# A two-block network on one core: the expert layers' token state made in the weights' feature order, its three bf16 parts written without a step

## The reference, cut to what matters

```python
# block 1
hx = _modulate(_rms_norm(x, g_pre_ffn[l]), mx[3], mx[4])
x = x + mx[5] * _rms_norm(_moe_ffn(hx, ...), g_post_ffn[l])     # 64 experts, top 8, width 256, and a shared one
# block 2
h2 = rms_norm(x, norm2_g[l]) * (1 + scale2) + shift2
x = x + gate2 * hier_moe(h2, ...)                                # 4 groups x 8 experts, top 2, width 512
# both: with s the tokens of expert e
y = (jax.nn.silu(xb @ we_gate[e]) * (xb @ we_up[e])) @ we_down[e]
```

## Time and profile before

| | us |
|---|---|
| Median of 3 runs | 1755.04 (1752.9 to 1756.14) |
| Span of the profiled execution (its own time is given by its span alone) | 1752.8 |
| TensorE products busy | 1413.3 (81%) |
| VectorE busy | 386.8 (22%) |
| ScalarE busy | 261.3 (15%) |
| Mixer of block 1, to the end of its w_out products | 0 to about 328 |
| Entry of layer 1, to the first gather | about 328 to 380 |
| Expert loop of layer 1 | 395 to 937 |
| Tail of layer 1, mixer of block 2 | 937 to 1222 |
| Entry of layer 2, to the first gather | 1222 to 1266 |
| Expert loop of layer 2 | 1273 to 1740 |

### The profile page before, as it was taken

The page is one execution under the profiler, slowest core; times in us unless marked ns, Lnnn a source line. Parts: engine busy times, 40 slices in busy tenths (PEclk is TensorE's granted clock), DMA queues, the critical chain, the costliest instruction groups (busy, mean ns, idle before and its releaser), DMA issues.

```text
span 1752.8 us, 19020 instructions
## 1 busy us (share of the span) xinstructions
PE 1413.3 (81%) x7683; PEld 667.6 (38%) x7683; DVE 386.8 (22%) x918; ACT 261.3 (15%) x420; POOL 96.6 (6%) x128
## 2 busy tenths in 40 slices
PE   4988688669999999999998599897566666566655
PEld 2636244334444444444444374443321222122211
DVE  1212887531111111111111313322410000000002
ACT  2002012171111111111111201010600000000001
POOL 1002960000000000000000000000000000000000
PEclk9999777889999999999999899999686887788877
DMA  9367574418999999999992362225189999999994
GB/s 376 145 236 276 220 306 161 197 48 354 370 367 374 360 374 358 364 371 355 378 356 119 133 245 101 96 96 233 55 352 421 421 421 422 422 422 422 422 421 189
DMA packets 86535, 515.38 MB, mean 294 GB/s; under 512 B 7760, under 2 KB 11192, under 8 KB 36440
## 3 DMA queue, kind: packets, MB, share of 16 engines
q1 hardware_dynamic: 84744, 509.24, 72.6%
q0 software_dynamic: 1520, 5.39, 0.9%
q10 hardware_dynamic: 224, 0.09, 0.0%
HBM read 513.63 MB, written 1.06 MB: 294 GB/s over the span
## 4 chain that ended last, share of the span: by engine, by line
PE 63%; DMA 21%; DVE 8%; ACT 4%; issue 2%; SPq 1%; DVEq 0%; ACTq 0%
PE PS L1135 15%; DMA W<-in_w_expert_down 10%; DMA W<-in_w_expert_up 9%; PE PS L1160 9%; PE PS L1118 7%; PE PS L1105 6%; PE PS L883 5%; PE PS L1298 3%; ACT scr L722 3%; PE PS L836 2%; PE PS L1258 2%; PE PS L1040 2%; PE PS L1356 2%; PE PS L1341 2%; PE PS L1268 2%
## 5 line engine op out<-in xcount | busy, mean ns | idle before, releaser
L1135 PE MATMUL PS<-W,scr 128*64 128x512 f32 (+1 forms) x2048 | 405.3, 731 | 126.0 <-DMA W<-in_w_expert_up 63.0
L1135 PEld LDWEIGHTS PS<-W,scr 128*64 128x64 f32 (+1 forms) x2048 | 114.6, 144 | 408.6 <-issue 259.4
L1160 PE MATMUL PS<-W,scr 128*64 128x512 f32 (+1 forms) x1024 | 186.8, 646 | 35.1 <-DMA W<-in_w_expert_down 33.5
L1761 DVE TENSOR_TENSOR scr<-scr,PS 128x256 f32<-128x256 f32 (+1 forms) x40 | 27.7, 693 | 691.5 <-PE PS L1135 386.5
L1118 PE MATMUL PS<-scr 128*128 128x512 f32 x336 | 155.4, 605 | 4.9 <-ACT scr L744 2.6
L1105 PE MATMUL PS<-scr 128*128 128x128 bf16 x2016 | 123.2, 222 | 23.5 <-ACT scr L722 23.5
L1105 PEld LDWEIGHTS PS<-scr 128*128 128x128 bf16 x2016 | 119.7, 100 | 26.7 <-issue 26.2
L1160 PEld LDWEIGHTS PS<-W,scr 128*64 128x64 f32 (+1 forms) x1024 | 51.0, 131 | 139.8 <-issue 93.1
L733 ACT COPY scr<-PS 128x512 f32<-128x512 f32 x80 | 46.9, 586 | 356.1 <-PE PS L1105 356.1
L1118 PEld LDWEIGHTS PS<-scr 128*128 128x128 f32 x336 | 60.4, 189 | 100.5 <-issue 96.5
L744 ACT COPY scr<-PS 128x512 f32<-128x512 f32 x80 | 42.9, 589 | 223.4 <-PE PS L1160 223.4
(11 more groups left out here) (395 smaller groups left out, 1214.6 us busy)
## 6 DMA issues: line engine op xcount, KB each, us to landing
W<-in_we_gate SPq DMA_DIRECT2D x66, 1024.0 KB, 6.8
W<-in_we_up SPq DMA_DIRECT2D x66, 1024.0 KB, 8.9
W<-in_we_down SPq DMA_DIRECT2D x66, 1024.0 KB, 7.2
W<-in_w_expert_gate SPq DMA_DIRECT2D x64, 1024.0 KB, 18.5
W<-in_w_expert_up SPq DMA_DIRECT2D x64, 1024.0 KB, 19.1
W<-in_w_expert_down SPq DMA_DIRECT2D x64, 1024.0 KB, 19.1
W<-in_w_ada SPq DMA_DIRECT2D x12, 4096.0 KB, 13.9
W<-in_w_in SPq DMA_DIRECT2D x6, 4096.0 KB, 16.9
```

The costliest lines, as they stand in the source:

```text
L1135: m = mm(dst if L == 2 else dst.rearrange("s (c n) -> s c n", c=2), hTe[:, k, j * cap:(j + 1) * cap], view[:, j, kk, :] if L == 2 else vie ...
L1160: m = mm(PS[6 + h][j * cap:(j + 1) * cap, :], aT[:, c, j * cap:(j + 1) * cap], view[:, j, cc, h * 512:(h + 1) * 512], start=(c == 0), stop ...
```

## The change

The order is made earlier. The transposes at the entry of both expert layers, and the products that make the columns of items 3 and 4, read every eighth feature (`every_kd`), so that chunk k of hT, of the shift and of the scale holds the features p*8 + k. A step of 8 fp32 elements is 32 bytes. The entry of block 2's mixer (n == 1) keeps the old order. hs_quarter and left become plain stretches of 512. ScalarE casts two parts rather than three; the third is written by DVE's second subtraction itself (`low_of_h`), with bf16 as its result, and the first gather waits for it by hs_left. Router and shared weights come in the new order too. The gains and the shifts' biases of the expert layers no longer come as rows that TensorE turns round, but by four DMAs of 32-byte pieces into ffn_cols, issued on SP behind the row biases and counted in row_loaded (112 becomes 176).

```diff
+def every_kd(ap):
+    return ap.rearrange("t (p k) -> t k p", k=KD)
...
-        hs_quarter = [[hs[:, part, n // 2, :].rearrange("t (k p) -> t p k", k=KD)[:, n % 2 * 64:n % 2 * 64 + 64, :] for n in range(4)]
-                      for part in range(3)]
-        left = [xn[:, n // 2, n % 2 * 512:n % 2 * 512 + 512].rearrange("t (p k) -> t p k", k=KD) for n in range(4)]
+        hs_quarter = [[hs[:, part, n // 2, n % 2 * 512:n % 2 * 512 + 512] for n in range(4)] for part in range(3)]
+        left = [xn[:, n // 2, n % 2 * 512:n % 2 * 512 + 512] for n in range(4)]
...
+                    for at, n_of, ap in ((FFN_SHIFT1, 2, A["b_ada"][0][3 * D:5 * D]), (FFN_SHIFT2, 2, A["b_ada_2"][0][3 * D:5 * D]),
+                                         (FFN_G1, 1, A["g_pre_ffn"][0]), (FFN_G2, 1, A["norm2_g_2"][0])):
+                        sp.dma_start(ffn_cols[:, at:at + n_of, :], ap.rearrange("(s p k) -> p s k", s=n_of, k=KD)).then_inc(S["row_loaded"], 16)
...
-                    sp.dma_start(sh_gu[:, :, 0:F1], rows(A["ws_gate"][0])).then_inc(loaded, 16)
+                    sp.dma_start(sh_gu[:, :, 0:F1], long_rows(A["ws_gate"][0], KD)).then_inc(loaded, 16)
...
-            pool.dma_start(wr, A["w_router"][0].rearrange("(k p) n -> p k n", p=P)).then_inc(S["wr_loaded"], 16)
+            pool.dma_start(wr, A["w_router"][0].rearrange("(p k) n -> p k n", k=KD)).then_inc(S["wr_loaded"], 16)
...
-                        act.wait_ge(S["hs_left"], 8 * (L - 1) + 4 * (part - 1) + n + 1)
-                    a.copy(hs_quarter[part][n], PS[n][:].rearrange("t (p k) -> t p k", k=KD) if part == 0 else left[n]).then_inc(S["hs_part"], 1)
+                        act.wait_ge(S["hs_left"], 8 * (L - 1) + n + 1)
+                    a.copy(hs_quarter[part][n], PS[n][:] if part == 0 else left[n]).then_inc(S["hs_part"], 1)
...
-            pe.wait_ge(S["vec_loaded"], 16 * 16)
+            pe.wait_ge(S["vec_loaded"], 16 * 14)
...
+                    ffn = s in (3, 4)
                     for j in range(KD):
-                        last = mm(PS[5][:, 3 * j:3 * j + 3], ada_rows[:, j * P:(j + 1) * P], sel3, start=True, stop=True)
+                        part = every_kd(ada_rows[:])[:, j, :] if ffn else ada_rows[:, j * P:(j + 1) * P]
+                        last = mm(PS[5][:, 3 * j:3 * j + 3], part, sel3, start=True, stop=True)
...
-                        last = tr(PS[k // 2][:, (k % 2) * T + b * P:(k % 2) * T + (b + 1) * P],
-                                  src[:, b, k * P:(k + 1) * P], ident[:])
+                        part = src[:, b, k * P:(k + 1) * P] if n == 1 else every_kd(src[:, b, :])[:, k, :]
+                        last = tr(PS[k // 2][:, (k % 2) * T + b * P:(k % 2) * T + (b + 1) * P], part, ident[:])
...
-                pe.wait_ge(S["hs_part"], 12 * L)
+                pe.wait_ge(S["hs_part"], 8 * L)
+                pe.wait_ge(S["hs_left"], 8 * L)
...
-            dve.wait_ge(S["row_loaded"], 112)
+            dve.wait_ge(S["row_loaded"], 176)
...
-            def left_of_h(L, part):
+            def left_of_h(L):
 
                 for n in range(4):
-                    dve.wait_ge(S["hs_part"], 12 * (L - 1) + 4 * part + n + 1)
-                    step(v.tensor_tensor(left[n], PS[n][:].rearrange("t (p k) -> t p k", k=KD) if part == 0 else left[n],
-                                         hs_quarter[part][n], ALU.subtract),
-                         S["hs_left"], wait=False)
+                    dve.wait_ge(S["hs_part"], 8 * (L - 1) + n + 1)
+                    step(v.tensor_tensor(left[n], PS[n][:], hs_quarter[0][n], ALU.subtract), S["hs_left"], wait=False)
+
+            def low_of_h(L):
+
+                for n in range(4):
+                    dve.wait_ge(S["hs_part"], 8 * (L - 1) + 4 + n + 1)
+                    dve.wait_ge(S["hs_left"], 8 * (L - 1) + n + 1)
+                    step(v.tensor_tensor(hs_quarter[2][n], left[n], hs_quarter[1][n], ALU.subtract), S["hs_left"], wait=False)
```

38 lines of the change are left out of this document (19 added, 19 removed).

## The result

The changed kernel takes **1722.16 us** (median of 4 runs, 1722.09 to 1726.83) against 1755.49 (4 runs, 1752.9 to 1756.14) for the kernel before on the same chip: ratio **0.9831**, 95% interval 0.9809 to 0.9852. Forecast were 1730.2, with 1721 to 1746 as the range. The profiled execution has a span of 1720.3 us, 32.5 less than before; the sum had 24.8 less. So the direction and the places were right, and another 7.7 us came off, most of them not at the entries.

What follows compares the result with a forecast made beforehand. TensorE and the weights' DMAs hold most of the chain, with slow ScalarE casts at both entries. 1752.8 - 12.4 - 1.6 - 15.3 - 2.5 + 7.0 = 1728.0 us of span, 2.2 more for the run: 1730.2 us; range 1721 to 1746.

Steps and rivals of the forecast that it cites:

- The bound and where time can be gained: TensorE bounds layer 1's loop, DMAs layer 2's; time gained at both entries reaches the end at full value.
- Casts at 0.59 us: At both expert entries, ScalarE's casts without the 256-byte step take 0.59 us each instead of 2.76.
- Layer 1's entry, -14.0: Layer 1's gather starts right behind the shared gate-up, -12.4 us, and runs at full clock, -1.6.
- Layer 2's entry, -17.8: Layer 2's gather starts at 1250.5, -15.3 us, and runs mostly at the higher clock, -2.5.
- Both arrive together: Layer 2's entry: TensorE's clearing products end at 1250.5 and DVE's masks are ready at 1250.2.
- rival d: Layer 2's entry stays at the low clock: gather 5.2 us, first gate-up products at half speed; 1736 us, chance 0.1.
- Stepped loads, +7.0: TensorE's 80 stepped loads on the path, in transposes and sums, cost 0.087 us more each, +7.0 us.
- Rival (a): TensorE's stepped loads in transposes and sums cost nothing; 1723.2 us, chance 0.25.
- (b): Entry casts stay slow because of their type, not the step; 1745.1 us, chance 0.07.
- (c): TensorE becomes the slow reader, 0.69 us a stepped load; 1768 us, slower than before, chance 0.08.
- DMAs at the start, and DVE's wait for them: nothing: Four more small DMAs on SP's queue at the start hold it up 5 to 10 us, but cost nothing.

## Why the prediction was right, point by point

- **The bound and where time can be gained.** Right. In layer 1's loop TensorE is busy for 540.48 of 541.6 us, as before, and the last stretch, layer 2's loop and what follows, is 0.9 us longer. So both entries' gains of 33.4 us reached the end but for these 0.9.
- **Casts at 0.59 us.** Right: 0.60 and 0.62. With the step put back they take 2.7 again, so the step was all of it, which the sum had assumed.
- **Layer 1's entry, -14.0.** -14.6. The masks are ready 5.6 us before TensorE is (364.8 against 370.4); I had 3.9 in hand.
- **Layer 2's entry, -17.8.** -18.75. "Both arrive together" holds to 0.37 us. The clearing products took 5.23 us instead of the 6.36 that I left them. The clock was 0.50 ahead of them in both kernels, but came up sooner: it was 0.72 from 1231.5 to 1233.0 and 1.00 behind that, where the kernel before had 0.50 for the first 4.1 us of its 6.36. A shorter wait ahead is not the reason, since the kernel with the step back on the casts waits 5.14 us there and takes 5.20. The masks by DVE then ended the wait.
- **The low clock stays (rival d).** No: the gather took 2.84 us.
- **Stepped loads, +7.0.** This step is the one that failed, and that its total was nearly hit (the stretch lost 6.6) is luck. I priced 80 loads alike at 0.087 us, after DVE's stepped read. In truth the 32 of the transposes cost nothing (by this 2.8 us too much), the 48 of the sums cost 0.12 us each where the clock is high and less where it is low already (4.1 us against 4.2), and 2.5 us come from dips of the clock, a term that I hadn't and that was 0.0 in another trace. ada4's sum is longer too (3.97 us) and hidden, as forecast. The Trainium skill (TensorE: Matmul & The Clock Gate, section LDWEIGHTS) has a load cost by its columns alone; the 335 ns against 192 speak against that for products, while rows of transposes take the same time plain and stepped. The Trainium skill (SBUF — State Buffer, section Specifications) wants at least two hits in a line of 16 bytes for full bandwidth. The products fit that only in part: at the low clock the 16-byte step, with one hit, took 3.85 us against 3.21, but the 8-byte step, with two, took 3.55 already. The transposes don't fit it.
- **Rival (a), stepped loads free, 1723.2.** The time came out at its number, and it is wrong all the same: the start was early by 3.8 us and the middle shorter by 2.9, which covered the 6.6: luck, too. With the late start the changed kernel takes 1727.2 us (its second profiled execution), 3.0 below the forecast.
- **Rivals (b) and (c).** The casts aren't slow by their type. Rival (b) also had the entries 8.3 and 8.6 us shorter with the step left in; 5.2 and 3.3 were measured, since DVE's bf16 writes were slow as well. And a load of 0.24 us is far from the 0.55 at which TensorE's steps would eat the gain.
- **DMAs at the start, and DVE's wait for them: nothing.** Right. The four DMAs hold SP's queue up by 6.7 us (35.76 to 42.47), and DVE's new wait ends while its next work isn't due:

```profile
46.72 0.29 DVE L1431 TENSOR_SCALAR scr<-scr 128x256 f32<-128x256 f32 x1 [1.21 <-DMA ffn_cols<-in_norm_g]
...
52.85 0.88 DVE L1436 TENSOR_SCALAR scr<-PS,cols 128x256 f32<-128x256 f32 x2 [5.62 <-PE PS L892]
```

- **Not foreseen: layer 1's loop to layer 2, -2.9.** 2.2 of it are the first 128 projection products of block 2, 27.89 us instead of 30.12:

```profile
1010.32 30.12 PE L1258 MATMUL PS<-hT,W 128*128 128x256 f32 x128 [1.31 <-DVE hT L1687]
```

```profile
998.26 27.89 PE L1268 MATMUL PS<-hT,W 128*128 128x256 f32 x128 [1.31 <-DVE hT L1698]
```

Nothing in that code changed and the wait ahead is the same, 1.31 us; it is the clock. All six traces of the table above with the new entry have 829.1 to 829.2 here, and the kernel with the step back on the casts, with the same 27.89 us, has 830.0. That the shift of the dips makes it is my reading; no run isolates it, and of before there is one trace.

## What to carry to other kernels

A change of layout has to stand somewhere; look for the reader or writer that doesn't feel it. Here the same reordering cost 2.1 us for each ScalarE cast that writes bf16 256 bytes apart, 2 us for a row of 16 product loads at the high clock, and nothing in TensorE's transposes or in a copy that reads PSUM. And before a few microseconds are ascribed to an edit, compare stretches between fixed rows and look at the clock in each: in this kernel chance at the start alone is worth 5 us, in the stretch of the sums dips of the clock make up to 2.7, and a dip counts only where no wait follows that would have been there anyway.

## What the runs showed of the hardware that was not expected

- A step of 32 bytes in the loaded operand doubles the time of a row of fp32 products' loads (0.12 to 0.24 us each, with 3 columns moving) with DMAs at over 400 GB/s beside them or without. It leaves rows of fp32 transposes as they are (1.94 and 1.96 us for 16 beside such DMAs, 1.91 and 1.95 without). For products at the low clock steps of 8 and 16 bytes lie between (3.55 and 3.85 us, with 3.21 plain and 3.95 at 32 bytes).
- TensorE's clock was 0.97 over 3.8 us of stepped product loads and 0.50 behind them, with no idle time; behind plain sums of 1.95 us it stayed at 1.00. The products behind took 29.3 to 29.6 us in six traces with the step and 27.8 to 27.9 in six without. It fell during stepped product loads with no DMA beside them too (0.66 over them, 0.50 behind), and not during transposes. At 0.50 the stepped loads take the same 0.24 us.
- ScalarE reads fp32 from PSUM 32 bytes apart at full speed (588 and 588 ns for 512). DVE writes bf16 256 bytes apart as slowly as ScalarE does (2.56 against 0.68 us).
- The same program starts differently from one execution to the next: with a stretch at the low clock at about 32 to 38 us or without, ada3's sum came 5.2 us apart (126.34 and 131.49). The other stretches agree to 0.2 us between these two traces. Over the twelve traces that sum started between 124.6 and 131.5 us. For the runs without a trace, 1722.1 to 1722.2 three times and 1726.8 once, this is an inference from their distance.
